# First norm of a hybrid encoder step: scales per tile, tiles 4 and 6 on GpSimd and ScalarE, another order on ScalarE and SyncE

## The reference

```python
def rmsnorm(x, g):
    x32 = x.astype(jnp.float32)
    y = x32 * lax.rsqrt(jnp.mean(x32 * x32, axis=-1, keepdims=True) + EPS)
    return y.astype(x.dtype) * g

h = rmsnorm(x, norm_mix)
(a_b, a_c, a_x, qb, kb, vb, qc, kc, vc, qi, ki, wi, g_a, g_b, g_c) = jnp.split(h @ w_in, SPLIT_POINTS, axis=-1)
...
x = x + merged @ w_out
```

## Time and profile before

| | us |
|---|---|
| median of 3 runs | 1852.12 |
| lowest and highest run | 1848.47, 1852.28 |
| the profiled execution: time | 1849.62 |
| the profiled execution: span of its core | 1847.8 |
| busy in the span: PE, DVE, ACT, POOL | 1776.8, 1203.7, 701.5, 571.4 |

### The profile page before, as it was taken

The page is one execution under the profiler, slowest core; times in us unless marked ns, Lnnn a source line. Parts: engine busy times, 40 slices in busy tenths (PEclk is TensorE's granted clock), DMA queues, the critical chain, the costliest instruction groups (busy, mean ns, idle before and its releaser), DMA issues.

```text
span 1847.8 us, 31461 instructions
## 1 busy us (share of the span) xinstructions
PE 1776.8 (96%) x12113; PEld 1723.4 (93%) x12113; DVE 1203.7 (65%) x2060; ACT 701.5 (38%) x1198; POOL 571.4 (31%) x454
## 2 busy tenths in 40 slices
PE   5999999999999999998999999999999999999997
PEld 4999999989999998777889998999999999999997
DVE  6256868878788876778955449766666666533232
ACT  4233112358811124876743343333333334221222
POOL 2111212256633323321231104555545553000000
PEclk9999999999999999999999999999999999999998
DMA  4111111110111113211214111222222223433112
GB/s 149 35 35 35 46 35 48 43 39 24 41 40 51 40 38 93 70 41 41 52 55 149 46 46 35 82 81 82 81 70 81 82 82 132 148 107 93 45 35 96
DMA packets 180176, 121.18 MB, mean 66 GB/s; under 512 B 9084, under 2 KB 165004, under 8 KB 180044
## 3 DMA queue, kind: packets, MB, share of 16 engines
q1 hardware_dynamic: 179068, 117.37, 21.3%
q0 software_dynamic: 976, 2.00, 0.4%
HBM read 101.45 MB, written 17.89 MB: 65 GB/s over the span
## 4 chain that ended last, share of the span: by engine, by line
PE 83%; DVE 8%; issue 3%; ACT 2%; POOL 2%; DMA 1%; SPq 0%; DVEq 0%; POOLq 0%; ACTq 0%
PE ps L1150 35%; PE ps L1502 20%; PE ps L1553 14%; PE ps L1259 3%; PE ps L1162 3%; PE ps L1282 3%; PE ps L1397 2%; PE ps L1357 2%; DVE probs L2405 1%; DVE key_mask L2220 1%; DVE top L2220 1%; DVE mix_lo L2576 1%; ACT probs L1798 0%; DVE t L2265 0%; DVE mix L2567 0%
## 5 line engine op out<-in xcount | busy, mean ns | idle before, releaser
L1150 PE MATMUL ps<-h_hi,w_hi 128*128 128x352 f32 (+1 forms) x936 | 206.4, 329 | 3.9 <-POOL w_lo L911 3.9
L911 POOL TENSOR_TENSOR w_lo<-w_raw,w_hi 128x1024 fp32r<-128x1024 f32 (+1 forms) x53 | 100.5, 1896 | 353.9 <-ACT w_hi L1583 353.9
L1150 PE MATMUL ps<-h_hi,w_lo 128*128 128x352 f32 (+1 forms) x936 | 202.6, 324 | 0.0
L1150 PE MATMUL ps<-h_lo,w_hi 128*128 128x352 f32 (+1 forms) x936 | 202.5, 325 | 0.0
L2220 DVE MAX8 top<-key_mask 128x8 f32<-128x768 f32 (+5 forms) x192 | 170.4, 889 | 11.8 <-PE ps L1150 1.2
L2220 DVE MATCH_REPLACE8 key_mask<-top,key_mask 128x768 f32<-128x768 f32 (+5 forms) x192 | 167.7, 876 | 0.9 <-issue 0.9
L1150 PEld LDWEIGHTS ps<-h_hi,w_hi 128*128 128x128 f32 (+1 forms) x936 | 158.8, 189 | 6.6 <-issue 4.9
L1150 PEld LDWEIGHTS ps<-h_hi,w_lo 128*128 128x128 f32 (+1 forms) x936 | 160.5, 187 | 0.5
L1150 PEld LDWEIGHTS ps<-h_lo,w_hi 128*128 128x128 f32 (+1 forms) x936 | 159.5, 188 | 0.5
L1583 ACT ACTIVATE w_hi<-w_raw 128x1024 fp32r<-128x1024 f32 (+1 forms) x86 | 80.3, 935 | 184.7 <-PE ps L1553 110.6
L1502 PE MATMUL ps<-mix_hi,quarter_hi 128*128 128x264 f32 x672 | 137.6, 286 | 4.5 <-ACT x_one L1583 1.9
(11 more groups left out here) (306 smaller groups left out, 4407.7 us busy)
## 6 DMA issues: line engine op xcount, KB each, us to landing
w_raw_in_lo<-in_w_in SPq DMA_DIRECT2D x56, 256.0 KB, 2.9
w_raw<-in_w_in SPq DMA_DIRECT2D x54, 256.0 KB, 3.1
ffn_tiles<-t SPq DMA_DIRECT2D x44, 264.0 KB, 2.4
ffn<-ffn_tiles SPq DMA_DIRECT2D x44, 264.0 KB, 4.2
w_raw<-in_w_gate SPq DMA_DIRECT2D x44, 256.0 KB, 3.1
w_raw<-in_w_up SPq DMA_DIRECT2D x44, 256.0 KB, 3.1
w_raw<-in_w_down SPq DMA_DIRECT2D x32, 256.0 KB, 3.0
w_raw_in_lo<-in_w_in SPq DMA_DIRECT2D x44, 128.0 KB, 2.2
```

The lines of the kernel that those rows point to most:

```text
L911: nc.gpsimd.tensor_tensor(WLO[:, k, 0:tiles, :], raw[:, k, 0:tiles, :], WHI[:, k, 0:tiles, :].bitcast(F32), ALU.subtract).then_inc(lo_read ...
L1150: last = nc.tensor.matmul(PS[0:rows, NB * k + b, 0:e - a], w[:, k, t, 0:rows], x[:, t, a:e], start=m == 0 and w is WHI and x is hi, stop=m ...
```

## The change

Five edits, all in the stage above:

- `X_BATCHES` has five batches: tile 0, tile 1, 2-3, 4-5 and 6-8. DVE's list is written out by hand.
- `SHARED_ROWS`: for tiles 4 and 6, POOL multiplies `XIN` by `NG` in place (it waits for that tile's square), and ACT multiplies the result by the scale, in a copy with a scale for each partition. DVE has no row product for them. POOL has the two multiplies among its powers: power 2, multiply 4, power 3, multiply 6, power 4.
- ACT's high halves follow two tiles behind the squares instead of five; the scaling of tile 4 stands behind square 6, that of tile 6 behind square 8, each ahead of a high half.
- ACT makes the high half of the first weight block ahead of high half 8 and of the tables' copies.
- SP issues the two loads of the first weight block behind tile 8 of x.

The arithmetic is the same but for the order of the two factors in tiles 4 and 6.

```diff
@@ -410,6 +410,7 @@
         taken = [sem("taken0"), sem("taken1")]
 
         x_in = [sem(f"x_in{k}") for k in range(NT + 1)]
+        x_rstd, x_weighted, h_rows_act = sem("x_rstd"), sem("x_weighted"), sem("h_rows_act")
         misc_in, x_sq, x_var, x_pow, h_rows, h_t, h_hi, h_lo = (
             sem(n) for n in ("misc_in", "x_sq", "x_var", "x_pow", "h_rows", "h_t", "h_hi", "h_lo"))
         const_ready, tables_t, tables_ready = sem("const_ready"), sem("tables_t"), sem("tables_ready")
@@ -654,7 +655,9 @@
             return range(NKV) if pair["sample"] else [pair["g"]]
 
 
-        X_BATCHES = [(0, 2), (2, 4), (4, 6), (6, NT + 1)]
+        X_BATCHES = [(0, 1), (1, 2), (2, 4), (4, 6), (6, NT + 1)]
+
+        SHARED_ROWS = (4, 6)
         R_IDX_C, R_IDX_W, R_IDX_K = 0, 1, 2
         R_B_C, R_B_V = 5, 7
         R_C_C, R_C_V = 10, 14
@@ -681,9 +684,8 @@
                 sp.dma_start(XIN[0:rows_of(i), i, :], x_rows(i)).then_inc(x_in[i], 16)
                 if i == 1:
                     sp.dma_start(NG[:, :], ins["norm_mix"].broadcast_to([P, D])).then_inc(ng_in, 16)
-                if i == 2:
-                    sp.dma_start(RAW[:, 1, 0:4, :], w_in[:, 0:4, C_QI:C_QI + P]).then_inc(raw_full[1], 16)
-                    sp.dma_start(RAW[:, 1, 4:8, :], w_in[:, 4:8, C_QI:C_QI + P]).then_inc(raw_full[1], 16)
+            for a in (0, KT // 2):
+                sp.dma_start(RAW[:, 1, a:a + KT // 2, :], w_in[:, a:a + KT // 2, C_QI:C_QI + P]).then_inc(raw_full[1], 16)
 
             def small(dst, src, s):
                 sp.dma_start(dst, src).then_inc(s, 16)
@@ -899,8 +901,20 @@
             def half(rows):
                 return ss[0:rows, 3, 0:1]
 
-            for m, (a, b) in enumerate(X_BATCHES):
+            def x_power(m):
+                a, b = X_BATCHES[m]
                 power((ss[:, 1, a:b], half(P).broadcast_to([P, b - a])), ss[:, 2, a:b], x_var, x_pow, m + 1)
+
+            x_power(0)
+            x_power(1)
+            pool.wait_ge(ng_in, 16)
+            x_power(2)
+            for i in SHARED_ROWS:
+                if i == 6:
+                    x_power(3)
+                pool.wait_ge(x_sq, i + 1)
+                nc.gpsimd.tensor_tensor(XIN[:, i, :], XIN[:, i, :], NG[:, :], ALU.mult).then_inc(x_weighted, 1)
+            x_power(4)
 
             for a in range(2):
                 load(KCI[:, a * HD:(a + 1) * HD], ins["cache_idx_k"][0, 0], side_in[0])
@@ -1167,7 +1181,10 @@
 
             for i in range(NT + 1):
                 r = rows_of(i)
-                pe.wait_ge(h_rows, i + 1)
+                if i in SHARED_ROWS:
+                    pe.wait_ge(h_rows_act, SHARED_ROWS.index(i) + 1)
+                else:
+                    pe.wait_ge(h_rows, i + 1 - sum(a < i for a in SHARED_ROWS))
                 if i >= 3:
                     pe.wait_ge(h_lo, i - 2)
                 for j in range(KT):
@@ -1621,15 +1638,21 @@
                     act.wait_ge(ss_clear, 1)
                 nc.scalar.activation(XJ[0:r, :], XIN[0:r, i, :], ACT.Square,
                                      accum_out=ss[0:r, 0, i:i + 1]).then_inc(x_sq, 1)
-                if i >= 5:
-                    h_high(i - 5)
-            for i in range(NT - 4, NT + 1):
-                h_high(i)
+                if i in (6, 8):
+                    shared, m = {6: (4, 3), 8: (6, 4)}[i]
+                    act.wait_ge(x_rstd, m + 1)
+                    act.wait_ge(x_weighted, SHARED_ROWS.index(shared) + 1)
+                    act.wait_ge(h_t, shared - 2)
+                    nc.scalar.activation(HN[:, shared % 3, :], XIN[:, shared, :], ACT.Copy,
+                                         scale=ss[:, 2, shared:shared + 1]).then_inc(h_rows_act, 1)
+                if i >= 2:
+                    h_high(i - 2)
+            h_high(NT - 1)
+            split(0, 0, 1)
+            h_high(NT)
             act.wait_ge(tables_t, 1)
             copy(VEC[:, 0:VEC_ROWS], PS[:, 6, 0:VEC_ROWS])
             copy(VEC[:, VEC_ROWS:VEC_ROWS + S_ROWS], PS[:, 6, P:P + S_ROWS]).then_inc(tables_ready, 1)
-
-            split(0, 0, 1)
 
             for n in range(1, J_A):
                 i, k = n // 2, n % 2
@@ -2119,8 +2142,6 @@
                 V_.tensor_tensor(H_LO[:, :, i * P:i * P + r], src,
                                  H_HI[:, :, i * P:i * P + r].bitcast(F32), ALU.subtract).then_inc(h_lo, 1)
 
-            done_low = 0
-
             def x_variance(m):
 
                 a, b = X_BATCHES[m]
@@ -2128,24 +2149,44 @@
                 V_.tensor_scalar(ss[:, 1, a:b], ss[:, 0, a:b], 1.0 / D, EPS,
                                  ALU.mult, ALU.add).then_inc(x_var, 1)
 
+            def x_scale(m):
+                a, b = X_BATCHES[m]
+                dve.wait_ge(x_var, m + 1)
+                rsqrt(P, ss[:, 1, a:b], ss[:, 2, a:b], x_pow, m + 1).then_inc(x_rstd, 1)
+                dve.wait_ge(x_rstd, m + 1)
+
+            def x_scaled(i):
+                if i >= 3:
+                    dve.wait_ge(h_t, i - 2)
+                r = rows_of(i)
+                V_.scalar_tensor_tensor(HN[0:r, i % 3, :], XIN[0:r, i, :], ss[0:r, 2, i:i + 1], NG[0:r, :],
+                                        ALU.mult, ALU.mult).then_inc(h_rows, 1)
+
             x_variance(0)
+            x_scale(0)
             dve.wait_ge(ng_in, 16)
-            for m, (a, b) in enumerate(X_BATCHES):
-                dve.wait_ge(x_var, m + 1)
-                step.mark(rsqrt(P, ss[:, 1, a:b], ss[:, 2, a:b], x_pow, m + 1))
-                step.wait()
-                for i in range(a, b):
-                    r = rows_of(i)
-                    if i >= 3:
-                        dve.wait_ge(h_t, i - 2)
-                    V_.scalar_tensor_tensor(HN[0:r, i % 3, :], XIN[0:r, i, :], ss[0:r, 2, i:i + 1],
-                                            NG[0:r, :], ALU.mult, ALU.mult).then_inc(h_rows, 1)
-                    if i == a and m + 1 < len(X_BATCHES):
-                        x_variance(m + 1)
-                    if i >= 2:
-                        h_low(i - 2)
-                        done_low += 1
-            for i in range(done_low, NT + 1):
+            x_scaled(0)
+            x_variance(1)
+            x_scale(1)
+            x_scaled(1)
+            h_low(0)
+            x_variance(2)
+            x_scale(2)
+            x_scaled(2)
+            h_low(1)
+            x_scaled(3)
+            x_variance(3)
+            h_low(2)
+            x_scale(3)
+            x_scaled(5)
+            h_low(3)
+            x_variance(4)
+            h_low(4)
+            x_scale(4)
+            x_scaled(7)
+            h_low(5)
+            x_scaled(8)
+            for i in range(6, NT + 1):
                 h_low(i)
 
             dve.wait_ge(misc_in, 16 * 7)
```

## The result

| | before | after |
|---|---|---|
| median of 7 runs, us | 1852.12 | 1855.84 |
| lowest and highest run, us | 1848.47, 1855.87 | 1854.09, 1857.44 |
| the profiled execution: time, span, us | 1849.62, 1847.8 | 1857.44, 1855.7 |
| first projection starts, us | 38.39 | 43.22 |

The changed kernel takes **1.0023** of the time of the one before, with a 95% interval of 1.0013 to 1.0034. On 1852 us that is 4.3 us more, between 2.4 and 6.3.

The account below looks back on a forecast made before the run. DVE's throughput was taken to bound the start, ahead of PE's first projection. A walk through the engines' hops put that at 42.2 against 38.39; +3.8 on a mean of 1850.6 gave 1854.4 us, range 1850.5 to 1858.0.

Parts of the forecast that it names:

- What bounds it: Start of the program: PE does only transposes ahead of 38.39, DVE's throughput bounds; a shift there moves the end one for one.
- Step 3: ACT's high halves two tiles behind: squares wait behind high halves that wait for transposes; DVE idle some 6 us.
- Step 2: Single scales for tiles 0 and 1: rows 0 at 7.68, 1.54 before 9.22, the norm row landing just in time.
- Step 4: GpSimd's products: multiply 4 takes 2.35 and holds DVE's row product of tile 3, which ends 1.0 late.
- Step 5: ACT's scaling of tiles 4 and 6: two more instructions of about 1.05, each ahead of a high half.
- Steps 1 and 6: First weights' loads behind x: tile 3 gains at most 1.84, or nothing; weights' high half ahead of the last: 1.36 gained.
- A: Rival: POOL does not hold DVE, rows 3 ends 1.0 sooner; +2.8, 1853.4; chance 0.1.
- B: Rival: TensorE's clock comes early, the first matmuls start fast, 2.1 us less; +1.7, 1852.3; chance 0.1.
- C: Rival: squares stay ahead of the transposes and DVE remains the bound; -5.3, or -4.3 with holding, 1846.3; chance 0.1.
- D: Rival: later than the walk, by held small scale operations or slower ACT scaling; +5.5, 1856.1; chance 0.1.
- the likeliest: Main case: first projection at 42.2 instead of 38.39, +3.8; chance 0.6.

Follow-up runs that it names:

- Experiment 1: Changed kernel with ACT's squares 5, 6 and 7 ahead of high half 2, square 8 ahead of high half 3; first projection 39.60, 1852.37 us, ratio 1.0009.
- experiment 4: Kernel before with high halves three tiles behind the squares instead of five, nothing else; first projection 43.38, 1854.06 us.
- experiment 3: Changed kernel with POOL's multiply 4 made to wait until DVE's row product of tile 3 is over; first projection 42.28, 1856.55 us.
- experiment 8: Changed kernel with the first weights' loads put back behind tile 2 of x; first projection 42.78, 1853.61 us.
- experiment 9: All parts of the change, three lists reordered so squares stay ahead; first projection 32.50, 1844.07 us, ratio 0.9963 against the kernel before.
- experiment 5: Kernel before with only the first weights' high half ahead of high half 8 and the tables' copies; first projection 36.68, 1848.35 us.
- experiment 2: Changed kernel without sharing: DVE makes the row products of tiles 4 and 6, high halves still two behind; first projection 43.05, 1853.05 us.
- experiments 1, 4 and 6: The sixth: kernel before with only the first weights' loads issued behind x; first projection 36.41, 1848.83 us. The other two have their own lines.
- the second of 10: Kernel of experiment 9 in another new order with nothing shared, DVE making all nine row products; first projection 33.11, 1846.72 us, ratio 0.9978.
- experiment 10: Two unshared kernels: the kernel before with single scales, moved loads and early weights' high half (35.33, ratio 0.9981); a new order (33.11, 0.9978).

## Why the prediction was right

The forecast was 1854.4 us by a walk of +3.8 at the first projection; measured were 1855.84 us, +4.83 at the projection and +4.3 in the medians. The time alone cannot tell 3.8 from 4.8, as its interval goes from 2.4 to 6.3; the timeline can. The forecast also stood on 1850.6 for the kernel before, whose median over seven runs is 1852.12. Point by point:

- **What bounds it.** PE's standing still ahead of 38.39, carried to the end one for one: held, by the windows and by the table above.
- **Step 3, the one that decides.** Foreseen: square 3 at 11.93, square 5 at 19.26, square 6 at 22.65, square 8 at 29.7, DVE idle some 6 us. Measured: 12.71, 20.16, 23.45, 30.55 and 5.97. Experiment 1 undid only this and took back 3.62; experiment 4 did only this to the old kernel and lost 4.99.
- **Step 2 was mis-sized.** The norm row was called "just in time" at 6.0 behind its issue; it took 6.6, and rows 0 stood at 8.38 instead of 7.68. This 0.7 lies at the head of the chain and is most of the 1.0 by which the start missed. The prediction had the row land at 7.68 and the product start at 7.68, with no margin between them; the landing deserved a range of its own.
- **Step 4.** Foreseen: the product of tile 3 ends 1.0 late. It took 2.25 for 1.28, and experiment 3 has 1.28 back. The multiply itself took 2.67, not 2.35: it began while DVE's row product of tile 2 (15.89, 1.29) was under way, and was held in its turn, since in after and in the experiments 1 and 8 it ended 2.21 to 2.24 us past the end of that product, 0.1 less than its own length. By the Trainium skill ("SBUF — State Buffer", Who interferes with whom), it is the order of issue and not the shape of the operation that decides which of the two is blocked; the runs agree from both sides, with 3.28 on DVE in experiment 3 and 3.33 on POOL in experiment 9.
- **Step 5 was mis-sized by 0.1 each.** The scalings took 1.14 and 1.15, not a square's 1.05. The Trainium skill ("ScalarE: Activation LUTs", What ACT_TABLE_LOAD costs) gives a pointer operand of one value a partition some 93 ns on top of an immediate one; the trace agrees with 0.09. What else is left of the 1.0 is the way from the last variance to its rsqrt, 1.21 from start to start (31.71 to 32.92) where the walk had 1.11. Low half 4 stands between them, and POOL's power takes 0.85 for three tiles instead of 0.70 for two; they end at 33.01 and 32.81, and the trace does not say which of them it was.
- **Steps 1 and 6.** Nothing for the moved loads in the changed order by way of tile 3 (experiment 8), 1.36 for the hoisted high half (experiment 5, 1.35). Held, but for the later norm row, if the moved loads are its cause.
- **The rivals.** A (no holding) falls with the 2.25, though experiment 2 shows that the sharing as a whole cost only 0.2 to 0.4. B (early clock) falls for this execution: the 24 transposes from 34.96 took 4.67 us, all at the slow pace, and the first matmuls were as slow as before. Its mechanism is real, though: transposes ran at the fast pace in several of the other kernels, and in the experiments 1, 4 and 6 that moved the start by 0.6 to 0.7. That it stayed out here is partly luck. C (faster) named the other order's worth quite well, -4.3 to -5.3: with the squares truly ahead the kernel of 9 and the second of 10 start 5.9 and 5.3 sooner. The sum behind it does not hold: C counted 2.4 for two products less on DVE, and the second of 10 has all nine there. D differs from the likeliest only in size, and the start at +4.83 lies between the two.

## What to carry to other kernels

In a list that runs strictly in order, the distance between an engine's own early work and the first instruction that waits for a later engine is a reserve. Shortening it may look free, as each instruction is as short as before, and turns a pipeline into a serial loop through every engine. Before moving work off the busiest engine, see whether it stays the busiest: here 2.4 us taken from DVE were worth less than the hold that came with them beside 6 us of waiting, and about one microsecond (0.6 to 1.2, not isolated) once the order was right. And where two engines meet on the same memory, a wait that avoids one meeting may only move the hold to the next one.

## What was not expected of the hardware

- A DVE instruction need not be long to be held. In after, a copy of two elements a partition (`sinks_sample`) took 1.80 and 2.24 us beside POOL's low halves of the weights, against 0.16 alone (in the kernel before one took 2.29, at 35.99), and in experiment 1 an rsqrt step of 128x2 took 1.15 against 0.16. Nobody waited for the copies.
- The granted-clock column says nothing up to its first change. It reads 1.00 in after for the first 45 us (the window above), while three projection matmuls take 1.08 us up to 47 and 0.65 from 47.53. From its first change on it agrees with the pace. In experiment 9 it is 0.50 in 34 to 36 us, and there three of the first matmuls take 1.08; it is 1.00 in 28 to 32, and there the eight transposes of the small tile take 0.65, against 1.06 in experiment 10. So ahead of the first change one must look at the pace of like instructions, not at the column.
- Transposes can run at either pace, and which one changed from kernel to kernel: the 24 in one piece at 34.96 in after stayed slow, in experiment 6 eight of the last took 0.68 us instead of 1.06. It is worth 0.6 to 0.7 us at the start of the first projection.
- The same wait of 1.94 us was followed by half a clock in some executions and not in others (0.57 against 1.00 in the result's section), worth 1.5 us.
- Landings of one and the same load, the third in its queue, lay between 5.7 and 7.0 us over 13 executions, and it is seen at the end of a chain that begins with it: 0.4 sooner in experiment 8 than in after, and the first projection 0.44 sooner.
